# Gate and up weights of a mixture-of-experts layer, loaded eight consecutive rows to a partition

## The reference

```python
h = rmsnorm(x, norm_w)                       # (2048, 1024)
g = argmax(h @ w_group)                      # one of 4 groups
top2 of (h @ w_expert) among the group's 8 experts, softmax weights
y = (silu(h @ w_gate[e]) * (h @ w_up[e])) @ w_down[e]
x = x + sum over the two experts of weight * y
```

## Time and profile before

| | us |
|---|---|
| median of 3 executions | 3409.23 |
| lowest and highest | 3402.83, 3414.1 |
| profiled execution, first to last instruction (span) | 3408.4 |
| profiled execution, its own time beside the span | not recorded |
| TensorE busy in the span | 2706.7 |
| VectorE busy | 1866.0 |
| ScalarE busy | 1479.5 |
| GpSimd busy | 699.9 |
| mean granted clock of TensorE, share of full | 0.890 |

### The profile page before, as it was taken

The page is one execution under the profiler, slowest core; times in us unless marked ns, Lnnn a source line. Parts: engine busy times, 40 slices in busy tenths (PEclk is TensorE's granted clock), DMA queues, the critical chain, the costliest instruction groups (busy, mean ns, idle before and its releaser), DMA issues. The chain is left out here.

```text
span 3408.4 us, 46743 instructions
## 1 busy us (share of the span) xinstructions
PE 2706.7 (79%) x12218; PEld 2156.9 (63%) x12219; DVE 1866.0 (55%) x3368; ACT 1479.5 (43%) x2040; POOL 699.9 (21%) x458
## 2 busy tenths in 40 slices
PE   5999969999799488988863994699599477899840
PEld 3777747777577366767643883588477366777630
DVE  3444434444466575455635666567466587545645
ACT  4444444444344244444423564365444244444423
POOL 0000000000011354444421001100011255433532
PEclk8999979999899699999985997799799688999975
DMA  3122221222543487777746113412444387777757
GB/s 106 62 68 74 68 74 62 68 74 68 190 137 129 157 276 269 247 261 265 261 149 218 43 49 129 148 49 80 153 137 134 106 310 268 273 255 266 267 203 259
DMA packets 341930, 546.29 MB, mean 160 GB/s; under 512 B 30193, under 2 KB 254081, under 8 KB 341889
## 3 DMA queue, kind: packets, MB, share of 16 engines
q1 hardware_dynamic: 296000, 384.81, 34.4%
q0 software_dynamic: 29616, 101.76, 8.7%
q10 hardware_dynamic: 16272, 59.25, 4.3%
HBM read 410.47 MB, written 135.30 MB: 160 GB/s over the span
## 5 line engine op out<-in xcount | busy, mean ns | idle before, releaser
L1285 POOL TENSOR_TENSOR experts_gu_lo<-experts_gu_raw,experts_gu_hi x64 | 385.7, 6027 | 160.6 <-ACT experts_gu_hi L1309 159.9
L118 PE MATMUL experts_ps<-experts_gu_hi,experts_hT_hi 128*128 (+1 forms) x760 | 331.7, 436 | 90.3 <-issue 70.2
L119 PE MATMUL experts_ps<-experts_gu_lo,experts_hT_hi 128*128 (+1 forms) x760 | 319.8, 421 | 0.0
L120 PE MATMUL experts_ps<-experts_gu_hi,experts_hT_lo 128*128 (+1 forms) x760 | 318.5, 419 | 0.0
L1366 DVE TENSOR_TENSOR experts_gu_lo<-experts_gu_raw,experts_gu_hi (+1 forms) x64 | 279.7, 4371 | 66.8 <-ACT experts_gu_hi L1309 66.8
L1309 ACT ACTIVATE experts_gu_hi<-experts_gu_raw (+1 forms) x128 | 238.0, 1907 | 91.2 <-DMA experts_gu_raw<-in_moe_w_up 31.9
L118 PE MATMUL route_ps<-route_w_hi,route_src_hi 128*128 128x512 f32 x512 | 216.2, 422 | 60.8 <-DVE route_w_lo L979 60.8
L118 PEld LDWEIGHTS experts_ps<-experts_gu_hi,experts_hT_hi 128*128 128x128 f32 x760 | 156.4, 206 | 140.2 <-issue 106.1
L118 PE MATMUL gla_ps<-gla_wvg_hi,gla_hT_hi 128*128 128x512 f32 x512 | 212.3, 415 | 0.0
L119 PE MATMUL route_ps<-route_w_lo,route_src_hi 128*128 128x512 f32 x512 | 209.9, 410 | 0.0
L120 PE MATMUL route_ps<-route_w_hi,route_src_lo 128*128 128x512 f32 x512 | 208.8, 408 | 0.0
(11 more groups left out here) (315 smaller groups left out, 6560.0 us busy)
## 6 DMA issues: line engine op xcount, KB each, us to landing
experts_gu_raw<-in_moe_w_gate SPq DMA_DIRECT2D x64, 1024.0 KB, 5.6
experts_gu_raw<-in_moe_w_up SPq DMA_DIRECT2D x64, 1024.0 KB, 10.6
experts_wd_raw<-in_moe_w_down SPq DMA_DIRECT2D x64, 1024.0 KB, 6.7
y_rows<-experts_y ACTq DMA_DIRECT2D x97, 512.0 KB, 6.3
gla_w_raw<-in_gla_w_in SPq DMA_DIRECT2D x18, 1024.0 KB, 6.7
y_rows<-gla_zeros POOLq DMA_DIRECT2D x8, 2048.0 KB, 8.4
route_src<-oT_rows SPq DMA_DIRECT2D x32, 512.0 KB, 4.5
x_rows<-route_x_new SPq DMA_DIRECT2D x32, 512.0 KB, 2.9
```

What stands on the lines that cost most here:

```text
L118: nc.tensor.matmul(out, w_hi, x_hi, start=first, stop=False)
L119: nc.tensor.matmul(out, w_hi, x_lo, start=False, stop=False)
L120: return nc.tensor.matmul(out, w_lo, x_hi, start=False, stop=last)
L1285: pool.tensor_tensor(gu_lo[:, slot(e), DVE_SHARE:], gu_raw[:, slot(e), DVE_SHARE:], gu_hi[:, slot(e), DVE_SHARE:].bitcast(F32), ALU.subtract)\
```

## The change

The weight rows that one partition takes are now eight consecutive ones: feature p*8+k stands in partition p at place k. In DRAM these are 8 KB in one run. In SBUF gate and up no longer share a row of 512 but have a plane each (`[P, 2 slots, 2 planes, 8, 256]`), so that these 8 KB are one run there too. The moving operand of a gate/up matmul is then two runs of 256 columns, one in each plane, and the splits cover two runs. The down weights are loaded as before. The router's weights follow the same order of features. So that `h` has this order too, the `Norm` of the route stages (and only theirs, `rows_of=8`) writes element p*8+k of a row to place k*128+p: the instruction reads side by side and writes with a step of 128 elements, eight at a time.

```diff
-    def __init__(self, m, k, x, h, square, depth=2):
+    def __init__(self, m, k, x, h, square, depth=2, rows_of=1):
...
-        nc.vector.scalar_tensor_tensor(out=self.h[:, j], in0=self.x[:, j], scalar=self.rstd[:, j:j + 1],
-                                       in1=self.norm_w[:], op0=ALU.mult, op1=ALU.mult)\
-            .then_inc(self.h_done, 1)
+        h, x, gain = self.h[:, j], self.x[:, j], self.norm_w[:]
+        if self.rows_of > 1:
+            h = h.rearrange("q (k p) -> q p k", k=self.rows_of)
+            x, gain = (v.rearrange("q (p k) -> q p k", k=self.rows_of) for v in (x, gain))
+        nc.vector.scalar_tensor_tensor(out=h, in0=x, scalar=self.rstd[:, j:j + 1], in1=gain,
+                                       op0=ALU.mult, op1=ALU.mult).then_inc(self.h_done, 1)
...
-        norm = Norm(m, k, x_new, h, square[:])
+        norm = Norm(m, k, x_new, h, square[:], rows_of=KD)
...
-                sp.dma_start(w_route[:, :, 0:GROUPS], w_group.rearrange("(k p) c -> p k c", p=P))\
+                sp.dma_start(w_route[:, :, 0:GROUPS], w_group.rearrange("(p k) c -> p k c", k=KD))\
...
-            sp.dma_start(w_route[:, :, GROUPS:], w_expert.rearrange("(k p) c -> p k c", p=P))\
+            sp.dma_start(w_route[:, :, GROUPS:], w_expert.rearrange("(p k) c -> p k c", k=KD))\
...
-        gu_raw = m.sb("gu_raw", [P, 2, KD, 2 * FF])
+        gu_raw = m.sb("gu_raw", [P, 2, 2, KD, FF])
...
-        gu_hi = m.sb("gu_hi", [P, 2, KD, 2 * FF], F32R)
-        gu_lo = m.sb("gu_lo", [P, 2, KD, 2 * FF], F32R)
+        gu_hi = m.sb("gu_hi", [P, 2, 2, KD, FF], F32R)
+        gu_lo = m.sb("gu_lo", [P, 2, 2, KD, FF], F32R)
...
-                load(e, gate_in, gu_raw[:, slot(e), :, 0:FF], w_gate)
-                load(e, up_in, gu_raw[:, slot(e), :, FF:], w_up)
+                load(e, gate_in, gu_raw[:, slot(e), 0], w_gate, "e (p k) c -> p e k c", KD)
+                load(e, up_in, gu_raw[:, slot(e), 1], w_up, "e (p k) c -> p e k c", KD)
...
-                pool.tensor_tensor(gu_lo[:, slot(e), DVE_SHARE:], gu_raw[:, slot(e), DVE_SHARE:],
-                                   gu_hi[:, slot(e), DVE_SHARE:].bitcast(F32), ALU.subtract)\
+                pool.tensor_tensor(gu_lo[:, slot(e), :, DVE_SHARE:], gu_raw[:, slot(e), :, DVE_SHARE:],
+                                   gu_hi[:, slot(e), :, DVE_SHARE:].bitcast(F32), ALU.subtract)\
...
-                nc.scalar.activation(gu_hi[:, slot(e), at], gu_raw[:, slot(e), at], ACT.Copy)\
+                nc.scalar.activation(gu_hi[:, slot(e), :, at], gu_raw[:, slot(e), :, at], ACT.Copy)\
...
-                nc.vector.tensor_tensor(gu_lo[:, slot(e), 0:DVE_SHARE], gu_raw[:, slot(e), 0:DVE_SHARE],
-                                        gu_hi[:, slot(e), 0:DVE_SHARE].bitcast(F32), ALU.subtract)\
+                nc.vector.tensor_tensor(gu_lo[:, slot(e), :, 0:DVE_SHARE], gu_raw[:, slot(e), :, 0:DVE_SHARE],
+                                        gu_hi[:, slot(e), :, 0:DVE_SHARE].bitcast(F32), ALU.subtract)\
...
-                    last = matmul3(nc, ps[:, GU], hT_hi[:, c], hT_lo[:, c], gu_hi[:, slot(e), c],
-                                   gu_lo[:, slot(e), c], c == 0, c == KD - 1)
+                    last = matmul3(nc, ps[:, GU], hT_hi[:, c], hT_lo[:, c], gu_hi[:, slot(e), :, c],
+                                   gu_lo[:, slot(e), :, c], c == 0, c == KD - 1)
```

More of the change, by code:

```diff
@@ L230 @@
 class Norm:
-    def __init__(self, m, k, x, h, square, depth=2):
+    def __init__(self, m, k, x, h, square, depth=2, rows_of=1):
         self.x, self.h, self.eps, self.square, self.depth = x, h, k.eps, square, depth
+        self.rows_of = rows_of
         self.norm_w = m.sb("norm_w", [P, D])
@@ L1235, in _, with load @@
             sp.dma_start(ids[:], ids_dram.rearrange("(p n) o -> p (n o)", p=P)).then_inc(ids_in, DMA)
-            def load(e, landed, into, w):
+            def load(e, landed, into, w, layout, rows):
                 if not (isinstance(e, int) and e == 0):
                     sp.wait_ge(landed, nth_dma(e - 1))
-                sp.dma_start(into, w[bass.ds(e, 1)].rearrange("e (k p) c -> p e k c", p=P)).then_inc(landed, DMA)
+                sp.dma_start(into, w[bass.ds(e, 1)].rearrange(layout, k=rows)).then_inc(landed, DMA)
             def load_gu(e):
-                load(e, gate_in, gu_raw[:, slot(e), :, 0:FF], w_gate)
-                load(e, up_in, gu_raw[:, slot(e), :, FF:], w_up)
+                load(e, gate_in, gu_raw[:, slot(e), 0], w_gate, "e (p k) c -> p e k c", KD)
+                load(e, up_in, gu_raw[:, slot(e), 1], w_up, "e (p k) c -> p e k c", KD)
             def load_wd(e):
-                load(e, wd_in, wd_raw[:, slot(e)], w_down)
+                load(e, wd_in, wd_raw[:, slot(e)], w_down, "e (k p) c -> p e k c", KF)
             load_gu(0)
```

## The result

The changed kernel takes 3422.14 us (median of 6 runs, 3418.25 to 3423.57) against 3409.36 us before (6 runs, 3402.83 to 3414.1): a ratio of 1.0039, 95% interval 1.0027 to 1.0050, so slower by 12.8 us. The forecast was 3421. The profiled execution of the changed kernel has a span of 3420.6 us and a time of its own of 3422.15 us.

The account below looks back on a forecast made before the run. TensorE was busy 83 to 84% of the edited stages, so its waits counted; a route turn ran through VectorE for one tile, TensorE for the other. Terms +16 − 2 − 2 = +12 us gave 3421 us, range 3397 to 3433.

Parts of the forecast that it names:

- 15 × 1.07 = 16 us: Route stages: strided norm write takes 1.07 us more per instruction, exposed 15 times, 16 us in all.
- The price from the read alone (0.74): Route norm: lower price of the strided write, 0.74 us each, from L1000, which reads with a 32-byte step.
- 13 loop waits and two tails: Route stages: longer write exposed at 7 and 6 short TensorE waits, plus one long wait ending each stage.
- Sum: +16 − 2 − 2: Whole kernel: strided write +16 us, first gate/up pairs −2, gathers −2, together +12 us.
- the −4 us: Experts stages: 2 us from first gate/up pairs landing sooner, 2 us from gathers landing earlier.
- The forecast's upper end, 3428: Whole kernel: top of the forecast's own range 3413 to 3428, meant as no DMA gain.
- The terms at nothing: Router weights, splits in two runs, and gate/up matmuls reading two runs of 256 columns: each taken as 0.
- Rival 1: Route norm: strided write is free, only −4 us is left, 3405 us; chance 0.30.
- Rival 2: Experts stages: longer load packets delay each gather by 1.8 us, 29 us in all, around 3450 us; chance 0.07.
- Rival 3: Experts stages: loads free 27 us; 3382 us with a free write, 3398 with its cost; chance 0.08.
- Rival 4: Gate/up matmuls' two-run operand or GpSimd's two runs cost up to 46 us, about 3440 to 3455; chance 0.05.

Follow-up runs that it names:

- e8: Kernel before, four norms reading first input in steps of 8, 16, 512 and 32 bytes (gla, lru, route, finish), output wrong; norms took 1285 to 2080 ns.
- e4: Changed kernel with the contiguous norm of before; TensorE's transposes read every eighth column instead; 3406.24 us, ratio 1.0002 to the kernel before.
- e5: Kernel before with an extra contiguous VectorE addition ahead of each route norm; 3423.20 us, ratio 1.0039.
- e3: Changed kernel with norm and router weights of before; ScalarE makes a permuted copy of h for the store; 3406.94 us, ratio 0.9999 to the kernel before.
- e2: Changed kernel with only the planes kept: old feature order, 1 KB pieces, contiguous norm; 3408.72 us, ratio 0.9998 to the kernel before.
- e1: Changed kernel with gate and up side by side in SBUF again, so loads land in 1 KB pieces; 3429.91 us, ratio 1.0068 to the kernel before.
- e6: Changed kernel with eight unused identity transposes ahead of the router's waits in all tiles; 3413.14 us, ratio 1.0007 to the kernel before.
- e10: New loads, contiguous norm, transposes reading every eighth column, plus eight unused identity transposes in even tiles; 3399.79 us, ratio 0.9970 to the kernel before.
- e9: New loads, contiguous norm, transposes reading every eighth column, plus eight unused identity transposes in all tiles; 3398.99 us, ratio 0.9969 to the kernel before.
- e11: Kernel before with eight unused identity transposes ahead of the router's waits in even tiles; 3397.06 us, ratio 0.9965.

## Why the prediction came out right

**The write costs a wide step's price, and is exposed once in a turn.** Right in mechanism. The size of the term was made of 15 × 1.07 = 16 us. The price is 0.79 us, so L1766, the row that I followed for having a stepped write, misled: its operation steps both sides. (Its 1.0 ns per element is also 1.02 us for 1024, not 1.07.) The price from the read alone (0.74) was nearer, and e8 shows that a read and a write cost the same. The exposure was put at 13 loop waits and two tails. Measured are six VectorE tiles a stage, at 0.72 us each in the mean, 4.3 us a stage; why a tile grows by a little less than the write was not looked into. The tail was put at the long wait for `route_both`; that one did not grow, but the last tile's wait for `h` just ahead of it did, by 0.7 us. Together that is 10 us for both stages.

**What the sum left out** is the clock. The prediction named the waits of TensorE and did not ask what a longer wait does to the work after it. Its own row had the sign: 0.88 of the clock in the stage. The TensorE tiles of 17.7 us are 4.3 us of the first loop's growth and 4.7 of the second's, 9 us together, about as much as the write itself. With the 10 us of the write that is 19 of the 19.8 us by which the two stages grew. By the timed runs the write costs 12.6 us (0.37%, the changed kernel against e4) to 13.3 (0.39%, e5 against before), clock and all, so the stages of the profiles overstate it; how much of this is scatter from run to run was not resolved.

**"Sum: +16 − 2 − 2"**: the gains of the loads were taken too high. The first pair lands 0.9 us sooner, as forecast at 1.0, and the packets are down by 114,688, as forecast. But e3 and e4, which hold all of the loads' gain and none of the write's loss, stand at 0.9999 and 1.0002, and the −4 us lies just outside their intervals (down to −3.8 and −2.7 us). The gathers' 0.6 us sooner bought nothing: in the first experts stage rows cost TensorE 11.7 us after the start (33.4 less 21.7) where it was 9.4. The write term too high by 3 us against the timed runs and the loads' gain too high by up to 4 offset each other. By the stages of the profiles it is the other way round, +19.8 and −7.9 for the forecast's +16 and −4, and again the two misses offset. So 3421 was nearer than its parts, and that part of the hit is luck. (The forecast's upper end, 3428, is also 3 us above what its terms give: with no gain from DMA they sum to 3425.)

**The terms at nothing** held: router weights, splits (L1285 at 5738 ns, now 5740) and the two-run operand (gate and up matmuls 436/421/419 ns in the mean for L118, L119 and L120, now 433/418/416; e2 at 0.9998).

**The rivals.** Rival 1 (a free write) falls with 2.07 us. That it decides below 0.3 us was not tried. Rival 2: a packet did get longer. From 1180 to 1740 us the load queue has these rows, before and after:

```profile
q1 hardware_dynamic: 70763, 95.14, 51.3%
```
```profile
q1 hardware_dynamic: 17546, 98.22, 47.4%
```

That is 65 ns a packet (51.3% of 16 engines for 560 us over 70763) and then 242, a mean over the 8 KB packets and the down loads' 4 KB ones. So an 8 KB packet is at least near the 0.28 us that the rival assumed. Yet the gathers land in 7.1 us in place of 7.7; only the longest grew, from 10.0 to 10.7. Long packets in front did not delay the median gather, so the 1.8 us of the rival is refuted for this kernel; whether engines take turns packet by packet is not shown by that. Rival 3 (the loads free 27 us) falls with e3 and e4. Rival 4 falls with e2.

**What stays open.** In e1 the new order in 1 KB pieces costs some 8 to 10 us more than the same in 8 KB runs, at the edge of what the intervals can tell, and its experts stages are 3.0 and 4.2 us longer than before. Its pieces are as many and as long as those of before; only their order in DRAM and in the queue differs. No run separates the two. The second experts stage shrank in the changed kernel's profile by 6.6 us. With the new loads it has 571.4 us in e6, 575.3 in e3 and e4, 578.0 in e10 and 580.6 in e9; with the old ones 576.6 in e11, 581.7 in e2 and 581.8 in e5. The two ranges overlap, so two profiles do not settle what the loads do there.

## What to carry to other kernels

Price a stepped SBUF operand of VectorE before moving a permutation into it: at steps of 16, 32 and 512 bytes 1024 fp32 elements took 2.03 to 2.09 us in place of 1.285, for a read as for a write. Put a permutation on the engine whose work has cover at that place: here TensorE's weight load (e4) and ScalarE (e3) took it for free. When an edit lengthens short waits of TensorE, look at the granted clock of the steady part too: the wait may cost again in the matmuls behind it. And faster landings are worth what the wait that ends last in that stage gives back, which here was nothing that the runs resolve.

## What the runs showed of the hardware that was not expected

- One stepped operand costs VectorE the same whether read or written, and nearly the same at 16, 32 and 512 bytes (2031 to 2088 ns); 8 bytes cost nothing (1285 and 1286).
- ScalarE takes about as long for the permuting copy: 2072 ns with a 512-byte write step and a contiguous read, where its activation over 1024 contiguous elements (L249) takes 1.06 us.
- TensorE's weight load of an fp32 tile with a 32-byte step takes 193 ns in place of 141, 0.4 ns more for each of 128 elements, where VectorE loses 0.73 to 0.78 and ScalarE's copy about 1.0 against L249.
- Eight useless transposes in a wait of 1.1 us raise the granted clock of the steady part from 0.96 to 1.00 and make the kernel before 0.35% faster (e11).
- The loop has a third rhythm. In e1, whose route stages have the changed kernel's code, the second stage has waits of 0.74 and 0.29 us in alternate tiles, and a loop of 228.6 us where the first has 231.3. The second route stage of e5 has a loop of 228.6 us too, with VectorE idle for 0.65 us before `x_new` as in e1. From e1:

```profile
2516.93 1.95 PE L1158 MATMUL route_ps<-route_w_route,route_hT 128*128 128x36 f32 x16 [0.74 <-DVE route_both L1017]
...
2532.90 1.95 PE L1158 MATMUL route_ps<-route_w_route,route_hT 128*128 128x36 f32 x16 [0.29 <-DVE route_both L1017]
```
